# Where the side work stands in a doubling inverse: from ahead of a level's last product to between its two halves

## The reference, cut to what matters

```python
kb = kc * bc[..., None]
a_mat = jnp.where(strict, jnp.einsum('bhnid,bhnjd->bhnij', kb, kc) * dmat, 0.0)
rhs = jnp.concatenate([vc * bc[..., None], kb * jnp.exp(gc)[..., None]], axis=-1)
sol = lax.linalg.triangular_solve(a_mat + jnp.eye(l), rhs, left_side=True, lower=True, unit_diagonal=True)
...
# per chunk, and for the samples (one token each) in the same way
s = s * gl[..., None, None] + jnp.einsum('bhck,bhcv->bhkv', k_i, v_new)
```

## Time and profile before

| | |
|---|---|
| median of 3 runs | 1587.48 us (1587.34 to 1589.97) |
| the profiled execution | 1588.4 us, of which the profile's span is 1586.7 us |
| granted TensorE clock, mean | 0.997 |
| busy: PE, DVE, ACT, POOL | 1555.7, 1061.8, 883.2, 249.4 us |
| HBM | 156 GB/s over the span |

### The profile page before, as it was taken

One profiled execution on the slowest core, in us unless ns is written; L12 is line 12 of the kernel. 1 busy time (PEld: TensorE's weight loads), 2 busy tenths in 40 slices (PEclk: granted clock), 3 DMA queues, 4 the chain that ended last, 5 costly groups with the idle time before them and its releaser, 6 DMA issues.

```text
span 1586.7 us, 37805 instructions
## 1 busy us (share of the span) xinstructions
PE 1555.7 (98%) x16228; PEld 1476.4 (93%) x16228; DVE 1061.8 (67%) x1736; ACT 883.2 (56%) x1704; POOL 249.4 (16%) x314
## 2 busy tenths in 40 slices
PE   9999999999999999999999999999999999999997
PEld 7998799999997999999788888999999997999997
DVE  7966677745757867547793747775569847867643
ACT  6856656633645666434652546665358548666433
POOL 7105350000110200003003420200010025400000
PEclk9999999999999999999999999999999999999999
DMA  9940465565754665553634103665569612555540
GB/s 253 286 140 30 134 180 174 182 205 181 245 160 134 199 181 183 195 186 94 190 97 140 24 7 93 181 186 186 186 171 265 184 55 77 178 180 183 187 165 28
DMA packets 245529, 250.10 MB, mean 158 GB/s; under 512 B 16270, under 2 KB 239284, under 8 KB 245300
## 3 DMA queue, kind: packets, MB, share of 16 engines
q1 hardware_dynamic: 237204, 224.78, 46.1%
q0 software_dynamic: 8016, 22.86, 4.9%
q10 hardware_dynamic: 144, 0.05, 0.0%
HBM read 229.75 MB, written 18.32 MB: 156 GB/s over the span
## 4 chain that ended last, share of the span: by engine, by line
PE 90%; DVE 5%; ACT 4%; issue 1%; DVEq 0%; POOL 0%; ACTq 0%; POOLq 0%
PE ps L851 86%; PE ps L855 3%; DVE tri L2786 1%; ACT vk L2074 1%; DVE mvs L2786 1%; ACT acts L2074 1%; DVE acts L2794 0%; DVE w_mlstm L2786 0%; ACT hn L2074 0%; DVE acts L2786 0%; ACT tri L2074 0%; DVE hn_split L2794 0%; DVE krow_r L2794 0%; ACT L2077 0%; PE ps L1817 0%
## 5 line engine op out<-in xcount | busy, mean ns | idle before, releaser
L2786 DVE TENSOR_TENSOR w_mlp<-ring,w_mlp 128x1024 fp32r<-128x1024 f32 x256 | 311.5, 1223 | 120.2 <-ACT w_mlp L2074 114.0
L2074 ACT ACTIVATE w_mlp<-ring 128x1024 fp32r<-128x1024 f32 x256 | 269.3, 1054 | 207.9 <-PE ps L851 207.9
L851 PE MATMUL ps<-hn_split,w_mlp 128*128 128x264 f32 x3072 | 373.3, 284 | 0.0
L851 PE MATMUL ps<-h_split,w_mlp 128*128 128x264 f32 x3072 | 372.6, 283 | 0.0
L851 PEld LDWEIGHTS ps<-hn_split,w_mlp 128*128 128x128 f32 x3072 | 372.1, 188 | 0.3
L851 PEld LDWEIGHTS ps<-h_split,w_mlp 128*128 128x128 f32 x3072 | 371.6, 188 | 0.0
L2074 ACT ACTIVATE tri<-ps 128x264 f32<-128x264 f32 (+4 forms) x222 | 101.3, 463 | 180.3 <-PE ps L851 155.9
L851 PE MATMUL ps<-gdn_hi,w_gdn 128*128 128x264 f32 x896 | 165.7, 285 | 0.0
L851 PEld LDWEIGHTS ps<-gdn_hi,w_gdn 128*128 128x128 f32 x896 | 139.3, 188 | 0.8 <-issue 0.8
L2786 DVE TENSOR_TENSOR tri<-tri 128x264 f32<-128x264 f32 (+4 forms) x145 | 59.6, 412 | 101.1 <-ACT h_split L2074 100.3
L851 PE MATMUL ps<-mixer_lo,w_gdn 128*128 128x264 f32 x448 | 126.9, 283 | 0.0
(11 more groups left out here) (459 smaller groups left out, 2646.9 us busy)
## 6 DMA issues: line engine op xcount, KB each, us to landing
ring<-in_ffn_w_dram SPq DMA_DIRECT2D x128, 1024.0 KB, 5.4
ring<-in_gdn_w_in_dram SPq DMA_DIRECT2D x32, 1024.0 KB, 7.5
ring<-in_ml_w_in_dram SPq DMA_DIRECT2D x12, 1024.0 KB, 5.6
ring<-in_rw_w_rkv_dram SPq DMA_DIRECT2D x12, 1024.0 KB, 4.9
st<-in_state_gdn_S_dram POOLq DMA_DIRECT2D x2, 4096.0 KB, 23.5
ring<-in_gdn_w_out_dram SPq DMA_DIRECT2D x8, 1024.0 KB, 5.0
out_gdn_S_s_dram<-st SPq DMA_DIRECT2D x16, 512.0 KB, 6.9
st<-in_state_mlstm_C_dram POOLq DMA_DIRECT2D x1, 4096.0 KB, 20.3
```

What stands on the lines that cost most here:

```text
L851: return nc.tensor.matmul(out, lhsT, rhs, start=start, stop=stop)
L2074: return nc.scalar.activation(out, in_, f, bias=bias, scale=scale)
L2786: return nc.vector.tensor_tensor(out, in0, in1, op)
```

## The change

On TensorE, the fills of levels 1 to 5 that stood behind T1 (key (l, 1)) stand behind P0 (key (l, 2)): `token_major(0)` in level 1, half an outer product, `token_major` and the other half in levels 2 to 4, and the outer products 3 and 4 in level 5. On ScalarE, `value_rows` of levels 1 to 4 moves with them, from behind t1 to behind n0. `sample_squares` stays behind t1. No instruction is added or removed, and the fills of VectorE and GpSimd stay as they are.

```diff
                 fills = {(0, 0): sample_products, (0, 1): spread_queries, (1, 0): sample_outputs,
-                         (1, 1): lambda: token_major(0), (1, 3): sample_norm}
+                         (1, 2): lambda: token_major(0), (1, 3): sample_norm}
                 for c in range(1, 4):
-                    fills[c + 1, 1] = lambda c=c: token_major_and_outer(c, c - 1)
-                fills[5, 1], fills[5, 3] = lambda: (outer_products(3), outer_products(4)), lambda: outer_products(5)
+                    fills[c + 1, 2] = lambda c=c: token_major_and_outer(c, c - 1)
+                fills[5, 2], fills[5, 3] = lambda: (outer_products(3), outer_products(4)), lambda: outer_products(5)
                 invert64(fills, X6, M6, Z6, PX6)
...
                 for l in range(1, 5):
                     fills[l, 0] = lambda l=l: scale_states(3 + l, 0)
-                    fills[l, 1] = lambda l=l: value_rows(l - 1)
+                    fills[l, 2] = lambda l=l: value_rows(l - 1)
                     fills[l, 3] = lambda l=l: scale_states(3 + l, 1)
-                fills[1, 1] = lambda: (sample_squares(), value_rows(0))
+                fills[1, 1] = sample_squares
```

## The result

The changed kernel takes 1591.24 us (median of 20 runs) against 1588.95 us before (20 runs): a ratio of 1.0015, 95% interval 1.0009 to 1.0021. It is slower by 2.3 us, or 1.4 to 3.3 us by the interval. That lies within 0.2%, as forecast, but the sign is clear of no change, where +0.4 us was forecast, and 1591.24 us lies outside the range of 1585.8 to 1590.2 us. The distance to the forecast of 1587.9 us is 3.3 us. About 1.5 us of it is the yardstick: the median of before was 1587.48 us over 3 runs and is 1588.95 us over 20. The other 1.9 us is what the change cost beyond the forecast.

What follows compares the result with a forecast made beforehand. TensorE, with 90% of the chain, was taken as the bound. First inverse +0.04 to +0.49 us and second -0.12 to +0.33 us, taken together as +0.4, made 1587.48 into 1587.9 us; range 1585.8 to 1590.2 us.

Steps and rivals of the forecast that it cites:

- The bound and the removed stall: Inverses: TensorE bounds the kernel; S0's 0.45 us stall behind ScalarE's n0, queued after value_rows, would go.
- The period: One level's loop in the inverse would take 5.58 to 5.73 us instead of 5.90, gaining 0.17 to 0.32 us.
- the lag from t0 to P0: From ScalarE's t0 to TensorE's P0 within a level: put at 0.1 to 0.25 us, nearer to the first.
- Level 2: P0 ahead of the fill would wait about 1.1 us for VectorE's subtraction, making V 1.57 us later.
- the lag behind VectorE's subtraction: Level 2: P0 would begin 0.05 us behind VectorE, as the transposes did behind keys, at 149.92.
- Level 5: VectorE's steps were to end about half a us ahead of P0, leaving P0 no VectorE wait in the sum.
- The sum of the inverses: First inverse +0.04 to +0.49 us, second -0.12 to +0.33 us; together -0.1 to +0.8 us, taken as +0.4 us.
- The 0.16 us that the second inverse was given as a start: Second inverse's level 2 took 6.49 instead of 6.33 us before, so the change was to start from 0.16 more.
- such stalls as a rival: Bank waits of outer products and additions late for solve_keys: 0.5 to 1 us an inverse, 1589 to 1589.5 us; chance 0.15.
- The clock: Waits of about 1.1 us in level 2 and 0.8 us before sample_norm would not lower TensorE's clock; no cost.
- the prediction's own signs of being wrong: Clock below 1.00 in either inverse, S0 of level 3 before 152.6, or periods of 5.45 us.
- the second rival: The clock falls in level 2, losing about 1.5 us each time, 3.0 + 0.4 us in all: 1590.9 us; chance 0.05.

Runs made afterwards that it cites:

- e3: The changed kernel with TensorE's fills moved but value_rows left ahead of n0 on ScalarE; ratio to before 1.0042.
- e4: The changed kernel with level 5's outer products 3 and 4 back behind T1; ratio to before 1.0004.
- e5: The change in levels 3 and 4 only, with the fills of levels 1, 2 and 5 as before; ratio to before 0.9994.
- e7: The changed kernel with the second half of VectorE's masked values formed behind its level 2 subtractions; ratio to before 0.9999.
- e0: The kernel before, run again with nothing edited and timed against itself; ratio 1.0001.
- e8: The kernel before with only VectorE's masked values split, the second half behind the level 2 subtractions; ratio to before 0.9998.
- e12: The kernel before with the whole change put into the first inverse only; ratio to before 1.0004.
- e14: A second look, one run, at the whole change in the first inverse only; that inverse's D length was 39.75 us, no ratio given.
- e11: The changed kernel run a third time with nothing edited; ratio to before 1.0020.
- e13: The kernel before with the whole change put into the second inverse only; ratio to before 1.0005.
- e1: The changed kernel run a second time with nothing edited; ratio to before 1.0020.
- e2: The changed kernel with level 2's TensorE fill and value_rows back behind T1 and t1; ratio to before 0.9999.
- e9: The changed kernel with VectorE's masked values split and level 5's outer products back behind T1; ratio to before 0.9992.
- e10: As e9, with ScalarE's second half of the scaling in levels 2 to 4 ahead of value_rows; ratio to before 0.9994.
- e6: The changed kernel with filler products on TensorE behind T1, three in level 2 and one in level 5; ratio to before 1.0023.

## Why the prediction was wrong

**The bound and the removed stall: right.** S0 of levels 3 to 5 no longer waits for ScalarE, and the loop through value rows, n1, c1 and t0 takes its place. The period was put at 5.58 to 5.73 us and is 5.60; the lag from t0 to P0 is 0.09 us, the lower end. e3 shows the loop from its other side.

**Level 2: right, a little small.** P0 was to wait about 1.1 us for VectorE and waited 1.09. It began at 151.56 - 1.44 = 150.12 us of before's time where 149.92 was said: the lag behind VectorE's subtraction is 0.24 us, not the 0.05 taken from the transposes. `sample_norm` waited 0.70 us and this died in level 2, as said. e4 against e5 shows that moving level 2's fill costs 0.9 us in the first inverse, and e7 that the wait that it makes is worth 1.1 us an inverse.

**Level 5: the step that failed in the sum.** "Q0 and the other VectorE steps end about half a us ahead of P0" does not hold behind level 4, where `sample_gates` comes ahead of the subtraction. P0 waited 0.34 us for VectorE, in a term that the sum put at nothing. It makes the last period 5.80 instead of 5.60 us. e4 shows that the outer products in front of P0 covered about 0.5 us.

**The sum of the inverses: too small.** First inverse: +0.51 us with the clock up (38.12 and 38.11 against 37.59, 37.62, 37.59 and 37.61 in executions whose first inverse is that of before), where +0.04 to +0.49 was said. It is about the lag of level 2 (0.2 us) and the wait of level 5 (0.2 us) on top of the lower end. Second: the mean of five is 38.50 (38.38, 38.77, 38.22, 38.22, 38.93), that of four unchanged ones 37.63 (37.73, 37.59, 37.58, 37.62), so +0.87 us, where -0.12 to +0.33 was said. The 0.16 us that the second inverse was given as a start was chance: S0 of level 3 waited 0.62 us for ScalarE in before and e5, and 0.45 us in e0, e8, e12 and e14. Together +1.4 us instead of +0.4. Part of the second inverse's +0.87 us are the stalls within S1: e11 and e13, which have none, give 38.22 us, +0.59, and the three with a stall of 0.41 to 0.78 us are 0.16 to 0.71 us longer. The prediction had such stalls as a rival (0.15), but not at this place.

**The clock: the other step that failed, priced at nothing.** "This is nearer to 0.97 than to 1.98, so I take no cost" looked at single waits. The clock did fall, in three of the ten inverses that have exactly the change (e1, e12, e14, all first inverses), at 3.3, 4.8 and 1.6 us, and in none of the eight that are exactly those of before. It is one of the prediction's own signs of being wrong, seen in e1 and not in the first changed execution. It did not fall in level 2, behind the long wait and the transposes, but behind level 5. The wait of level 2, right behind transposes, kept the clock at 1.00 in all ten, so the second rival, a fall there, did not come true; that its 1590.9 us lies nearest to the 1591.24 us measured is luck.

The premise was weak as well. All 18 executions have the wait of 1.97 or 1.98 us in front of the 16 transposes of the earlier trace rows. The granted clock fell behind it in 11 of them and stayed at 1.00 in seven, of which e2 is one; the transposes took 1.94 us there instead of 3.51:

```profile
805.36 1.94 PE L855 MATMUL ps<-ident,st 128*128 128x128 f32 x16 [1.98 <-DVE hn L2792]
```

So one trace was no ground for reading a yes or no off the length of a wait.

How much the clock carries can be read from all the runs, since each gives the mean granted clock of its whole span. It is 0.9961 over the 42 runs of the change (20, and 11 each in e1 and e11), and 0.9969 over the 115 runs of before that were timed beside the experiments; the difference is 0.0003 to 0.0014 by a 95% interval, found by drawing the runs anew many times. That is 1.4 us of withheld clock, and a straight line through both sets gives 0.64 us of time for each such us, so about 0.9 us. The rest shows in runs of equal mean clock (medians; every value of which there are at least three runs of each kernel):

| mean granted clock | before | change | longer by |
|---|---|---|---|
| 0.995 | 1590.45 us (16 runs) | 1591.93 us (3 runs) | 1.5 us |
| 0.996 | 1588.87 us (8 runs) | 1592.67 us (9 runs) | 3.8 us |
| 0.997 | 1588.80 us (50 runs) | 1590.23 us (13 runs) | 1.4 us |
| 0.998 | 1587.28 us (39 runs) | 1588.99 us (7 runs) | 1.7 us |

The straight line puts it at 1.9 us at equal clock. So some 1.4 to 1.9 us are the order's own length, and the two D give +1.4 us for it. With 0.9 us of clock that makes 2.3 to 2.8 us, where 2.3 us were measured in the first comparison and 2.4 to 3.2 us by the three ratios.

Over the 66 runs of e2, e4, e5, e7, e9 and e10, which take away one of the two waits or both, the mean clock is 0.9969, as before. But e6 closed both waits with filler and had 0.9956, and single executions of e9 and e3, which are other orders, had a fall at the same place. What in the order brings the falls is not settled.

What is shown: the waits of P0 for VectorE in level 2 and, smaller, in level 5 are where the inverses lose (e2, e4, e7). What stays open: why the clock falls more often with this order, about 0.9 us, and the stalls in S1 of the second inverse, about 0.3 us on average.

## What to carry to other kernels

Side work that stands in front of a step may be the cover of that step's own wait. Before moving it, ask for each level what the step would wait for with nothing in front, also for the engine whose order does not change; here the cover was worth 0.9 us in level 2 and 0.5 in level 5, and only the two levels between could spare it. A fall of the clock seen or not seen in one trace says little: count it over several executions, or compare the mean granted clock over many runs. Effects below 0.1% are better read as the length between two instructions, over several executions, than from a span or from a median of three runs.

## What the runs showed of the hardware

- The granted clock can fall without a long wait: in e12 it went to 0.50, the 1.2 GHz level, for 10.2 us, with no wait over 0.43 us in the 20 us ahead of it (level 2's 1.09 us ended at 150.99, the fall began at about 171.0) and two windows before it in which TensorE was busy 1.66 and 1.90 of 2.00 us. The work ahead of the fall was small float32 products and outer products on 32 rows; the unchanged inverses do the same work without a fall in any of eight.
- The same wait need not have the same effect: behind a wait of 1.97 or 1.98 us the clock fell in 11 of 18 executions.
- TensorE stands still for 0.26 to 0.78 us in the middle of a run of 64x64 products without waiting for anyone. It comes at recurring places of the stream, in some executions and not in others. In the stretch from 912 to 948 us the loads of instructions took 2.1% of the 16 DMA engines' time in e1 and 1.5% in e2, nine loads each (1.34 and 0.96 us apiece, worked out from 36 us times 16 engines), and R was 21.39 and 19.84 us. But e11 had 1.6% and R 21.03 us, so slow loads are at most a part of the cause, and no run shows that they are one.

```profile
q8 instruction: 9, 0.15, 2.1%
```

```profile
q8 instruction: 9, 0.15, 1.5%
```

The first line is the DMA queue of instruction loads of e1 over that stretch, the second that of e2: packets, MB, share of the 16 engines.
